# Two prompt tiles meet every expert as a dense product; the other rows still gather

## The reference

```
qry  = h @ w_query                        # 8 heads x 2 halves x 128
s    = qry . sub_keys                     # 128 scores per half
sv, si = top_k(s, 16)                     # per token, head and half
cand = sv[0][:, None] + sv[1][None, :]    # 16 x 16 sums
best, pos = top_k(cand, 16)               # eidx = si0 * 128 + si1 at pos
gate = softmax(best)
u, v = expert_u[eidx], expert_v[eidx]     # rows of 1024, out of 16384 experts
out  = sum over heads, picks of  gate * gelu(h . u) * v
```

## Time and profile before

| | before |
|---|---|
| median of three runs | 1859.97 us |
| span of the profiled execution (its own time) | 1860.3 us |
| PE busy | 1459.1 us, 78% |
| DVE busy | 1249.6 us, 67% |
| ACT busy | 688.9 us, 37% |
| POOL busy | 612.5 us, 33% |
| moved by DMA | 643.28 MB, of which 555.82 MB on the queue of the gathers |
| granted TensorE clock, mean | 0.838 |

### The profile page before, as it was taken

One profiled execution on the slowest core, in us unless ns is written; L12 is line 12 of the kernel. 1 busy time (PEld: TensorE's weight loads), 2 busy tenths in 40 slices (PEclk: granted clock), 3 DMA queues, 4 the chain that ended last, 5 costly groups with the idle time before them and its releaser, 6 DMA issues.

```text
span 1860.3 us, 22142 instructions
## 1 busy us (share of the span) xinstructions
PE 1459.1 (78%) x7786; PEld 684.7 (37%) x7786; DVE 1249.6 (67%) x2827; ACT 688.9 (37%) x1775; POOL 612.5 (33%) x590
## 2 busy tenths in 40 slices
PE   8999999999898896788877566666666676666666
PEld 4777878988544463333322101101111110000002
DVE  3077657886876658766767667777667677667665
ACT  3145455312444537524323222432322243222223
POOL 1100000000343244344345444454444444444442
PEclk9999999999999897799898767867666776676766
DMA  9533343206799999999999999999999999999997
GB/s 356 171 130 109 128 138 132 74 24 238 297 421 420 413 420 422 376 420 403 424 421 415 425 423 424 423 421 425 424 418 424 422 421 414 418 421 423 417 423 312
DMA packets 99903, 643.28 MB, mean 346 GB/s; under 512 B 11730, under 2 KB 11898, under 8 KB 31781
## 3 DMA queue, kind: packets, MB, share of 16 engines
q0 software_dynamic: 76912, 555.82, 72.3%
q1 hardware_dynamic: 22688, 85.96, 12.6%
q10 hardware_dynamic: 192, 0.09, 0.0%
HBM read 636.65 MB, written 6.18 MB: 346 GB/s over the span
## 4 chain that ended last, share of the span: by engine, by line
PE 40%; DMA 39%; DVE 9%; ACT 7%; issue 4%; POOL 1%; SPq 0%; ACTq 0%; DVEq 0%; POOLq 0%
DMA arena<-in_euv,consts 38%; PE abank L900 22%; PE dbank L900 5%; PE fsum L1635 4%; DVE arena L2368 4%; PE dbank L1635 4%; ACT consts L866 2%; POOL arena L473 1%; ACT L864 1%; ACT small L864 1%; PE fsum L964 1%; ACT L769 1%; ACT arena L746 1%; PE abank L1528 1%; ACT arena L490 1%
## 5 line engine op out<-in xcount | busy, mean ns | idle before, releaser
L2368 DVE CUSTOM_DVE_ANT_0 arena<-arena 128x1024 f32<-128x1024 f32 x520 | 633.8, 1224 | 399.8 <-DMA arena<-in_euv,consts 398.9
L473 POOL DMA_INDIRECT arena<-in_euv,consts x520 | 577.7, 1111 | 765.9 <-PE fsum L1635 370.1
L900 PE MATMUL abank<-arena 128*128 128x256 f32 (+4 forms) x2392 | 526.7, 378 | 5.1 <-ACTq L748 2.8
L1635 PE MATMUL dbank<-arena,consts 128*32 128x512 f32 x1024 | 360.6, 838 | 213.3 <-ACT consts L866 212.5
L900 PEld LDWEIGHTS abank<-arena 128*128 128x128 f32 (+1 forms) x2392 | 389.3, 191 | 161.6 <-issue 70.8
L1635 PE MATMUL fsum<-arena,consts 128*32 128x512 f32 x1024 | 298.9, 778 | 162.8 <-ACT consts L866 162.0
L864 ACT ACTIVATE small<-small 128x1 f32<-128x1 f32 x520 | 104.8, 202 | 675.4 <-DVE small L2368 669.6
L1635 PEld LDWEIGHTS dbank<-arena,consts 128*32 128x32 f32 x1024 | 42.0, 123 | 494.8 <-ACT consts L866 483.6
L490 ACT ACTIVATE arena<-abank 128x512 f32<-128x512 f32 (+5 forms) x228 | 111.7, 490 | 256.8 <-PE abank L900 243.9
L866 ACT ACTIVATE consts<-arena,small 128x32 f32<-128x32 f32 x520 | 167.1, 321 | 16.9
L1635 PEld LDWEIGHTS fsum<-arena,consts 128*32 128x32 f32 x1024 | 37.8, 120 | 365.1 <-ACT consts L866 346.5
(11 more groups left out here) (335 smaller groups left out, 1193.2 us busy)
## 6 DMA issues: line engine op xcount, KB each, us to landing
arena<-in_wstream SPq DMA_DIRECT2D x132, 512.0 KB, 5.7
arena<-in_euv,consts POOLq DMA_INDIRECT x520, 13.2
arena<-in_wout SPq DMA_DIRECT2D x8, 1024.0 KB, 9.5
arena<-in_x SPq DMA_DIRECT2D x5, 512.0 KB, 6.4
arena<-in_sdel POOLq DMA_DIRECT2D x1, 2048.0 KB, 9.6
out_deltas<-arena POOLq DMA_DIRECT2D x1, 2048.0 KB, 12.3
out_yp<-arena SPq DMA_DIRECT2D x4, 512.0 KB
arena<-mod SPq DMA_DIRECT2D x3, 512.0 KB, 11.1
```

The costliest lines, as they stand in the source:

```text
L473: pool.indirect_dma_start(ring[n % SLOTS], None, I["euv"], bass.IndirectOffsetOnAxis(cur[:, u % 2, c:c + 1], 0)).then_inc(ring_in[n % SLOT ...
L900: return pe.matmul(out, lhsT, rhs, start=first, stop=last)
L1635: last = pe.matmul(out[e][to:to + 32, :], weighed, v, start=h == 0 and kk == 0, stop=h == PH - 1 and kk == 3, skip_group_check=True)
L2368: TTR(uh, uh, rep[j] if t < NT else h2sb, 1.0, 0.0, ALU.mult, ALU.add, dot[:, n // NQ % 2, n % NQ:n % NQ + 1]).then_inc(s.dots_done, 1)
```

## The change

Tiles 0, 1 and the samples keep their gathers: `UNITS` is now 17 long and `TICKS` 132. Tiles 2 and 3 (`DT`, 256 tokens) are computed against all 16384 experts in 128 blocks of 128. For a block PE multiplies the block of u (a new input `ut`, u laid out with the model dimension on the partitions, 512 KB a block) with the transposed h of both tiles (`dense_scores`: eight products of 256 columns), ACT takes Gelu of the 128x256 result, DVE multiplies by the block's gates (`dense_gated`, 128x256), and PE multiplies with the block's v (`dense_values`: two tiles by two halves of 512 columns, accumulating in four PSUM banks over all blocks).

The gates are a table over (first key, second key, token). DVE keeps of each dense search the two key numbers and the gate (`chosen`), PE transposes them, and for every eight tokens DVE builds one-hot matrices by comparison with an iota (`hot`: one 128x1024 comparison and eight 128x128 compare-and-scale), PE multiplies them (`gate_table`: eight products of 128 columns) and ACT copies the result into a staging area (`stage`). Eight staged parts of 2 MB are written to a DRAM tensor `gd` and read back in groups of eight blocks (1 MB).

In the ticks: the sixteen queries take a tick each from 47 to 62; the 25 searches that come after tile 0's (tiles 1, 2, 3 and the samples) start every second tick from 52 to 94 and then at 100, 108 and 116, in three consecutive ticks each; `hot` has one set in each tick from 77 to 92 and two in each from 98 to 105; the dense blocks start at tick 107, four a tick, and the 28 blocks left after tick 131 follow the last one. At the end ACT and DVE close tiles 2 and 3 (`dense_end`). The rest of the diff moves buffers.

```diff
+GT, DT = 2, (2, 3)
+DTOK = len(DT) * P
+BLOCKS = 128
+BATCH, EIGHT, GROUP = 32, 8, 8
...
-        UNITS = [(t, h) for t in range(NT) for h in range(PH)] + [(NT, 0)]
+        UNITS = [(t, h) for t in range(GT) for h in range(PH)] + [(NT, 0)]
...
-        QUERY = {(47 + 2 * m if m < 8 else 64 + 3 * (m - 8)): m for m in range(2 * PH)}
+        QUERY = {47 + m: m for m in range(2 * PH)}
+        DENSE_SCORES = {52: (2, 0), 56: (2, 1), 60: (2, 2), 64: (2, 3), 66: (3, 0), 68: (3, 1), 70: (3, 2), 76: (3, 3)}
...
+        TWO_TICKS = {52: (1, 0), 54: (2, 0), 56: (2, 1), 58: (2, 2), 60: (1, 1), 62: (2, 3), 64: (2, 4), 66: (2, 5), 68: (1, 2), 70: (2, 6),
+                     72: (2, 7), 74: (3, 0), 76: (1, 3), 78: (3, 1), 80: (3, 2), 82: (3, 3), 84: (1, 4), 86: (3, 4), 88: (3, 5), 90: (3, 6),
+                     92: (1, 5), 94: (3, 7), 100: (1, 6), 108: (1, 7), 116: (NT, 0)}
+        for i in sorted(TWO_TICKS):
+            q = len(SEARCH)
+            SEARCH.append(TWO_TICKS[i])
+            for n, parts in enumerate(((0, 1), (2, 3), (4,))):
+                PIECES.setdefault(i + n, [])
+                PIECES[i + n] += [(q, p) for p in parts]
...
+        CHOSEN_AT = {75: 0, 97: 1}
+        HOT_AT = {77 + n: [n] for n in range(16)} | {98 + n: [16 + 2 * n, 17 + 2 * n] for n in range(8)}
+        DENSE_FROM, DENSE_EACH = 107, 4
+        def dense_at(i):
+            lo = (i - DENSE_FROM) * DENSE_EACH
+            return range(lo, min(lo + DENSE_EACH, BLOCKS)) if lo >= 0 else ()
...
+            def stage(n):                                            # ACT
+                b = n // (BATCH // EIGHT)
+                for half in range(2):
+                    t0 = n % (BATCH // EIGHT) * EIGHT + 4 * half
+                    if t0 == 0 and b >= 2:
+                        act.wait_ge(*second(gd_out[b % 2], 16 * (b // 2)))
+                    empty(staged[b % 2].rearrange("p (i t) -> p t i", t=BATCH)[:, t0:t0 + 4, :])
...
+            def dense_gelu(b):
+                if b >= 4:
+                    act.wait_ge(*second(v_used, b - 3))
+                empty(wd[b % 4], slice(0, DTOK), func=ACT.Gelu)
...
+            def gate_table(n):                                       # PE
+                pe.wait_ge(*second(ab_ready, n + 1))
+                for half in range(2):
+                    b = aring.to_fill()
+                    for q in range(4):
+                        last = mm(b[:, q * P:(q + 1) * P], hot_j[n % 2][:, 4 * half + q, :], hot_i[n % 2][:, 4 * half + q, :])
...
+            def dense_scores(b):
+                pe.wait_ge(*second(u_in[b % 4], 16 * (b // 4 + 1)))
+                bank = aring.to_fill()
+                for k in range(KT):
+                    last = mm(bank[:, 0:DTOK], uplace[b % 4][:, k * P:(k + 1) * P], h2T[1][:, k, P:P + DTOK], k == 0, k == KT - 1)
+            def dense_values(b):
+                pe.wait_ge(*second(v_in[b % 4], 16 * (b // 4 + 1)))
+                pe.wait_ge(*second(wd_ready, b + 1))
+                for i in range(2):
+                    for e in range(2):
+                        last = pe.matmul(dsums[i][e][:, :], wd[b % 4][:, i * P:(i + 1) * P], vplace[b % 4][:, 512 * e:512 * e + 512],
+                                         start=b == 0, stop=b == BLOCKS - 1, skip_group_check=True)
+            def dense(b):
+                if b == 0:
+                    pe.wait_ge(s.f_out, 1)
+                dense_scores(b)
+                if b >= 2:
+                    dense_values(b - 2)
...
+            for b in range(DTOK // BATCH):                           # SP
+                sp.wait_ge(*second(gs_ready, b + 1))
+                sp.dma_start(I["gd"][b], staged[b % 2]).then_inc(gd_out[b % 2].sem, 16)
...
+            for b in range(BLOCKS):
+                if b >= 4:
+                    sp.wait_ge(*second(ge_ready, b - 3))
+                sp.dma_start(uplace[b % 4], I["ut"][b]).then_inc(u_in[b % 4].sem, 16)
+                if b == 0:
+                    sp.wait_ge(*second(gd_out[1], 16 * (DTOK // BATCH // 2)))
+                    gates_group(0)
+                if b >= 4:
+                    sp.wait_ge(*second(v_used, b - 3))
+                sp.dma_start(vplace[b % 4], I["euv"][b * P:(b + 1) * P, D:2 * D]).then_inc(v_in[b % 4].sem, 16)
...
+            def hot(n):                                              # DVE
+                TT(hot_i[n % 2], bc(iota, 1, EIGHT), bc(of[:, 0, t0:t0 + EIGHT], 2, P), ALU.is_equal)
+                for t in range(EIGHT):
+                    made = TS(hot_j[n % 2][:, t, :], iota, of[:, 1, t0 + t:t0 + t + 1], of[:, 2, t0 + t:t0 + t + 1], ALU.is_equal, ALU.mult)
+            def dense_gated(b):
+                w = three(wd[b % 4], BATCH)
+                TT(w, w, gates_in[g % 2][:, :, BATCH * n:BATCH * (n + 1)], ALU.mult).then_inc(wd_ready.sem, 1)
```

More of the change, by code:

```diff
@@ L289, in replicated @@
         def replicated(i):
-            for t in range(NT - 1):
+            for t in range(GT - 1):
                 b = max(n for n, x in enumerate(TICKS) if x[1] == t)
@@ L349, in exp_at @@
[L349 to L357, removed]
-        def select_at(u, k):
-            return u + 1 < len(UNITS) and k == (3 if u == 0 else 2 if u + 1 == LATE else 0)
+            return None
+        SEARCH = [(0, h) for h in range(PH)]
@@ new lines, in build, with ended_search, exp_at @@
+        for i in sorted(TWO_TICKS):
[4 more added lines that the diff above has]
+                PIECES[i + n] += [(q, p) for p in parts]
+        def ended_search(q):
+            t = SEARCH[q][0]
+            n = len([x for x in SEARCH[:q + 1] if (x[0] in DT) == (t in DT)])
+            return second(dg_ready, n) if t in DT else (s.eg_ready, n)
+        def exp_at(i):
+            return [q for q, p in PIECES.get(i, ()) if p == 4]
@@ L363, in build @@
+        REST_OF_DENSE = [b for i in range(TAIL, TAIL + BLOCKS) for b in dense_at(i)]
         MEANS = []
@@ L856, in _ @@
             for i, (u, t, h, k) in enumerate(TICKS):
-                if exp_at(u, t, k) is not None:
-                    best_exp(exp_at(u, t, k))
+                for q in exp_at(i):
+                    best_exp(q)
                 if k == 0:
@@ L1514, in first_scores, with behind @@
+            def dense(b):
[4 more added lines that the diff above has]
+                    dense_values(b - 2)
+            def behind(i):
+                if i in CHOSEN_AT:
+                    chosen_turned(CHOSEN_AT[i])
+                for n in HOT_AT.get(i, ()):
+                    gate_table(n)
+                for b in dense_at(i):
+                    dense(b)
             def first_scores(half):
@@ L1651, in _ @@
                 woven(i)
-            pe.wait_ge(s.fs_ready, NT + 1)
+                behind(i)
+            for b in REST_OF_DENSE[:2]:
+                dense(b)
+            pe.wait_ge(s.fs_ready, GT + 1)
             b = aring.to_fill()
@@ L1657, in _ @@
             last.then_inc(s.aring_full, 1)
+            for b in REST_OF_DENSE[2:]:
+                dense(b)
+            for b in range(BLOCKS - 2, BLOCKS):
+                dense_values(b)
         @block.sync
@@ L1718, in _, with stored @@
                 load(n)
[L1719 to L1731, removed]
+            def stored(t):
+                sp.dma_start(O["yp"][t * P:(t + 1) * P, :], x_t[:, t, :]).then_inc(s.out_y, 16)
@@ L2380, in _ @@
                     square_sum(ended(i, 2))
-                for unit, piece in pieces(u, t, k):
-                    search(unit, piece)
+                for q, piece in PIECES.get(i, ()):
+                    search(q, piece)
                 if k == (5 if t < NT else 2) and u + 1 < len(UNITS):
                     gate_pattern(u + 1)
[L2385 to L2388, removed]
+                if ended(i, 4) == 0:
+                    finish(0)
+                if ended(i, 3) == 1:
+                    finish(1)
                 woven(i)
+                for x in HOT_AT.get(i, ()):
+                    hot(x)
+                for b in dense_at(i - 1):
+                    dense_gated(b)
+            for b in list(dense_at(TAIL - 1)) + REST_OF_DENSE[:2]:
+                dense_gated(b)
             finish_samples()
+            for b in REST_OF_DENSE[2:]:
+                dense_gated(b)
+            for i in range(2):
+                dense_end(i)
 def layout(a):
```

253 lines of the change are left out of this document (186 added, 67 removed).

## The result

The changed kernel takes 2246.35 us (median of four runs, 2245.19 to 2246.82); beside it the kernel before took 1860.15 us. The ratio is 1.2073, 95% interval 1.2056 to 1.2091. The profiled execution has a span of 2244.7 us. The forecast was 2210 us, range 2160 to 2290.

A forecast was written before the change was run, and what follows sets the result against it. It took the dense part as a PE bound and the crowded ticks before it mostly as DVE's: 1280 us to the first dense block, 917 dense, 11 end, 2 for handshakes, 2210 us; range 2160 to 2290 us.

The forecast's parts named there:

- dense part without it: From the first dense block on: PE bound, 885 us of blocks, 27 of slot products, 5 of remaining work, 917 us.
- the 2 for handshakes: Addition of 2 us to the sum for handshakes between the engines in 60 crowded ticks.
- The dense block: Each of 128 blocks: PE bound, 3.47 us of scores plus 3.44 us of values in f32, 6.91 us.
- Sixteen queries in sixteen ticks: Ticks 47 to 62: PE bound at 7.62 us a tick, 136 us in all where the old kernel took 94.
- the searches: Ticks 63 to 106: one search of 8.3 us of DVE starts every second tick, making DVE the bound; tick 107 at 1267 us.
- the first rival: Ticks 47 to 106 cost a chain of waits between engines, 1 to 2 us longer each: 2285 to 2330 us; 14%.
- Ticks 98 to 105: Two one-hot sets and an eighth of a search on DVE: 9.8 us a tick, 78 us, PE and ACT beside.
- The hand-over: Before the first dense blocks: last staging write, gate reads and loads in a row, 13 us, bounds 5 to 25.
- The clock: Dense part at granted clock 1.00; a 3% rival had it not hold, 2300 us for a tenth of the blocks.
- The searches did not hide: Rival: DVE's added work fits its idle holes, ticks 47 to 106 stay near the old: 2050 us or so; 4%.
- DMA did not stay the bound: Rival: dense products hide under 2.8 us of DMA a block, only bytes count: 1620 us; 3%.
- Two of the signs: Ticks 77 to 92: DMA share 0.6 or less; and DVE idle time in the crowded ticks would show the forecast wrong.

The follow-up runs named there:

- e1: Changed kernel with dense score products over 4 of the 8 parts of the model dimension, half of each score left out: 2030.34 us, ratio 1.0913.
- e2: Changed kernel with the dense products' operands turned into float16 in place by ACT and DVE: 1918.4 us, ratio 1.0306.
- e3: Changed kernel with ACT staging the gate table of ticks 98 to 105 in the same tick, not the next: 2225.32 us, ratio 1.1961.
- e5: Changed kernel with SP issuing two blocks of u before waiting for the last gates, and the samples' small loads after block 8: 2245.66 us, ratio 1.206.
- e6: Changed kernel with float16 dense operands, same-tick staging in ticks 98 to 105 and SP loading u two blocks ahead: 1818.17 us, ratio 0.9765.
- e4: Changed kernel with eight of the nine DVE instructions of each one-hot set left out: 2161.99 us, ratio 1.1622.
- e8: Changed kernel with ACT's staging copies writing contiguous columns, so gates stand in the wrong order: 2244.39 us, ratio 1.2061.

## Why the prediction held, and where it was off

By the steps of the forecast against the trace:

| step | forecast | measured |
|---|---|---|
| tick 47 starts | 764 | 766 |
| tick 63 | 900 | 901 |
| tick 77 | 999 | 999 |
| tick 93 | 1157 | 1155 |
| tick 98 | 1184 | 1181 |
| tick 106 starts | 1262 | 1287 |
| PE free for the first block | 1267 | 1298 |
| hole before the blocks | 13 | 22 |
| dense part without it | 917 | 913 |
| end | 11 | 11 |

(The 22 us are the 35.9 us from 1298.25 to the fourth scores at 1334.16, less three scores and one set of values, 13.9 us; the dense part is what is left up to the last product's end at 2233.5 us.)

The span is 35 us above the forecast of 2210, and it is no result of errors that cancel: 28 in ticks 98 to 105, 6 up to the first block, 9 in the hole, against 3 before tick 98, 4 in the dense part and the 2 for handshakes.

- *The dense block* was right: 6.89 us measured for 6.91. e1 shows that PE's products bound it, e2 that their price is that of f32. It is the step that decides the sign.
- *Sixteen queries in sixteen ticks* and *the searches* were right to a few us. A sum over the busiest engine was enough there; the first rival, a chain in place of the sum, is refuted for ticks 47 to 97 (PE 96% busy in ticks 47 to 62, DVE 94% to 98% from there to tick 97).
- *Ticks 98 to 105* were mis-sized: 9.8 us a tick by DVE's sum, 13.3 in the trace, 28 us over them, and PE was free for the first block 11 us after tick 106 began, for 5, as it had its last tables still to make. The step said that PE's tables and ACT's staging lie "beside". They do for one set a tick; with two sets, two one-hot buffers, two banks and staging a tick later they become a ring. This is the first rival's mechanism at another place than it named. e3 took 21 us out of it by moving the staging alone.
- *The hand-over* was mis-sized: 22 us for 13, inside its bounds of 5 to 25. The step took landings one behind the other as its price. The trace shows eight small loads of SP before the first u and full DMA engines, and e5 that taking the small loads away gains little; that the rest is bytes is argued. About 4 us of the 22 are the clock: after 14.48 us without work the first two sets of scores take 6.14 and 5.21 us at a granted clock of 0.59 and 0.71, where a later one takes 3.62.
- *The clock* held: 1.00 from 1355 to 2205 us. The searches did not hide, and DMA did not stay the bound in f32.

Two of the signs that the prediction named came out otherwise. DMA's share in ticks 77 to 92 is 0.70, not 0.6 or less, though its rate of 260 GB/s is 0.62 of 420. And DVE has idle time in ticks 98 to 105 (79 us busy of 106), which the prediction had called a sign of being wrong; for these ticks it was.

Four readings in it are slips that do not carry the sum. The pieces of a search add up to 8.4 us, not 8.3. The first rival, at 1 to 2 us for each of 60 ticks, begins at 2270 and not at 2285 us, and half of what it adds ends near 2270, not at the 2290 of the range; the measured time lies inside either. The 2.8 us for which PE waits in the earlier trace rows are one wait for ACT's scaling of h (L748), not for query copies. And in the earlier trace rows DMA is above a third in four of the first ten slices, 0.9 in the first.

Where the 384 us between the two spans lie, by the first L2368 and L2595 of the ticks: 41 us in ticks 47 to 62 (134.8 for 93.9), 20 in 63 to 76, 73 in 77 to 92 (155.9 for 82.9), 67 in 98 to 105 (106.1 for 39.5), some 4 elsewhere before tick 106, and from tick 106 on 957.7 us for 778.0, 180 more. Runs tested the dense part (e1, e2, e6) and ticks 77 to 92 and 98 to 105 (e3, e4, e8); the 61 us of ticks 47 to 76 are read from the profile alone.

## What to carry to other kernels

Trading gathered rows for dense products pays only if the engine that takes over the work has the time: 128 ticks of 5.0 us on DMA were given for 128 blocks of 6.9 us on PE, while the same block in float16 stays under its own DMA time. Price a block on each engine by rows of the same shape and type before the change. Where work for several engines is squeezed into a tick, adding each engine's work was enough here while every buffer pair was used once a tick; where one is used twice, draw the ring of who frees what, and when.

## What was not expected of the hardware

A copy of 128x512 f32 from PSUM by ACT takes 1.05 us when it writes columns 128 bytes apart and 0.60 us when it writes them side by side; the work is the same. That agrees in kind with the note on cachelines in the Trainium skill, "SBUF — State Buffer", section "Door 1: The DMA port swizzle" (16-byte lines, and a penalty for each access that crosses to a new one); no run here tried a distance between 4 and 128 bytes, so the mechanism is not shown.
